# The triangular inverse of RWKV-7 as diagonal 32x32 blocks: four 32x32 tiles of the array instead of two 64x64

## The reference, cut to what matters

```python
def step(s, inp):
    r_t, w_t, kk_t, b_t, k_t, v_t = inp
    sa = jnp.einsum('dbhvk,dbhk->dbhv', s, kk_t)
    s = s * w_t[..., None, :] - sa[..., :, None] * b_t[..., None, :] + v_t[..., :, None] * k_t[..., None, :]
    return s, jnp.einsum('dbhvk,dbhk->dbhv', s, r_t)
```

## Time and profile before

| | value |
|---|---|
| median of the runs shown | 2692.78 us |
| time of the profiled execution | 2691.81 us |
| its span, first to last instruction | 2689.8 us |
| mean granted TensorE clock | 0.961 |
| the five turns of RWKV (from the first product of the ladder's operands) | 457.5 to 796.0 us |
| PE busy share of the span | 91% |

### The profile page before, as it was taken

How to read it: one execution, slowest core, us unless ns; L and a number is a source line. 1 busy time by engine, 2 the same in 40 slices (tenths; PEclk the granted TensorE clock), 3 DMA queues, 4 the chain that set the end, 5 groups by cost and what they waited for, 6 DMA issues and landing times.

```text
span 2689.8 us, 74227 instructions
## 1 busy us (share of the span) xinstructions
PE 2448.0 (91%) x34058; PEld 1706.7 (63%) x34058; DVE 601.4 (22%) x1164; ACT 536.0 (20%) x1037; POOL 217.9 (8%) x243
## 2 busy tenths in 40 slices
PE   5899985999999769999999899998794999999998
PEld 3555564999994466777666345457453777766654
DVE  1113456666652330000000010106315000000001
ACT  3111043444421310000000036114413000000000
POOL 2000020333300010000000000003001000000000
PEclk8999997999999889999999999999896999999999
DMA  7665300000012269999999311110014999999970
GB/s 282 191 216 180 132 1 14 4 4 4 4 44 68 108 248 373 397 397 396 396 394 392 115 50 47 48 63 32 16 58 159 353 392 397 396 394 394 396 274 39
DMA packets 173468, 529.19 MB, mean 197 GB/s; under 512 B 23124, under 2 KB 27888, under 8 KB 173296
## 3 DMA queue, kind: packets, MB, share of 16 engines
q1 hardware_dynamic: 158688, 489.45, 48.1%
q10 hardware_dynamic: 10336, 24.21, 3.1%
q0 software_dynamic: 4272, 12.91, 1.4%
HBM read 506.75 MB, written 11.40 MB: 193 GB/s over the span
## 4 chain that ended last, share of the span: by engine, by line
PE 68%; issue 16%; DMA 5%; DVE 3%; ACT 2%; POOLq 1%; ACTq 1%; DVEq 1%; POOL 1%; SPq 0%
PE ps L1710 19%; PE ps L1725 17%; PE ps L1124 7%; PE ps L458 4%; PE ps L1840 4%; DMA big<-w_exp_down 3%; PE ps L1209 2%; PE ps L1912 2%; PE ps L1134 2%; PE ps L1908 2%; PE ps L460 1%; PE ps L830 1%; PE ps L438 1%; PE ps L1703 1%; PE ps L1196 1%
## 5 line engine op out<-in xcount | busy, mean ns | idle before, releaser
L1710 PE MATMUL ps<-rs,ring 128*64 128x80 f32 x12288 | 441.8, 233 | 5.8 <-issue 5.5
L1710 PEld LDWEIGHTS ps<-rs,ring 128*64 128x64 f32 x12288 | 429.9, 137 | 23.9 <-issue 23.0
L1811 DVE TENSOR_TENSOR big<-big,ps 128x320 f32<-128x320 f32 x64 | 28.3, 483 | 993.8 <-PE ps L1725 954.8
L1725 PE MATMUL ps<-big 128*80 128x512 f32 x512 | 226.4, 595 | 1.9 <-DMA big<-w_exp_down 1.5
L1725 PE MATMUL ps<-ring,big 128*80 128x512 f32 x512 | 225.0, 592 | 2.4 <-DVE big L1811 2.4
L555 PE MATMUL ps<-hT,ring 128*128 128x512 f32 x336 | 176.1, 606 | 11.1 <-ACTq L602 11.1
L1124 PE MATMUL ps<-big 64*64 64x64 f32 x5440 | 166.5, 219 | 16.9 <-DVEq L1095 16.9
L1781 ACT COPY big<-ps 80x512 f32<-80x512 f32 x64 | 34.1, 582 | 711.0 <-PE ps L1725 711.0
L1124 PEld LDWEIGHTS ps<-big 64*64 64x64 f32 x5440 | 163.1, 136 | 18.2 <-DVEq L1095 17.2
L1725 PEld LDWEIGHTS ps<-ring,big 128*80 128x80 f32 x512 | 76.6, 150 | 145.9 <-issue 141.8
L1725 PEld LDWEIGHTS ps<-big 128*80 128x80 f32 x512 | 74.3, 150 | 131.5 <-issue 129.8
(11 more groups left out here) (392 smaller groups left out, 3002.1 us busy)
## 6 DMA issues: line engine op xcount, KB each, us to landing
ring<-w_exp_up SPq DMA_DIRECT2D x124, 1024.0 KB, 10.8
ring<-w_exp_gate SPq DMA_DIRECT2D x68, 1024.0 KB, 12.1
big<-w_exp_down SPq DMA_DIRECT2D x64, 1024.0 KB, 11.3
ring<-w_exp_down SPq DMA_DIRECT2D x64, 1024.0 KB, 11.5
big<-w_exp_gate SPq DMA_DIRECT2D x60, 1024.0 KB, 10.6
big<-w_ada SPq DMA_DIRECT2D x22, 2048.0 KB, 8.7
ring<-w_in_odd SPq DMA_DIRECT2D x6, 2048.0 KB, 8.9
big<-big ACTq DMA_DIRECT2D x32, 256.0 KB, 6.4
```

The lines of the kernel that those rows point to most:

```text
L1710: last = nc.tensor.matmul(ps[2 * m + j // 4][a:a + HALF, (j % 4) * SLOTS:(j % 4 + 1) * SLOTS], ex_blocks[ex_slot(q)][:, k % 2, j * P + a:j ...
L1725: last = nc.tensor.matmul(ps[4 + f][0:SLOTS, :], hid[:, k, :], ex_blocks[ex_slot(q)][:, k % 2, f * W:(f + 1) * W], start=(k == 0), stop=(k ...
```

## The change

A diagonal 32x32 block of L is inverted by levels 1 to 4 alone; only level 5 joins two of them to 64x64. The change keeps L, X, XT, T1 and the masks as these diagonal blocks: four 32x32 blocks stand on the four quarters of the partitions (`QUARTERS`), 8 of them side by side, 256 columns in place of 512. Levels 1 to 4 run as `quarters`, 32 matmuls of 32x32 with 32 columns, on four tiles of the array in turn; `each` ran 16 of 64x64 with 64 columns. The pair products are formed as blocks from the start (`pair_quarters`): the two diagonal blocks of each matrix, and the corner block that only level 5 uses. At level 5 `corner_left` multiplies the corner with X (16 matmuls), ACT takes the product over with a minus sign, and `corner_right` (32 matmuls) makes the joined corner and, by an identity, moves the second diagonal block beside it; DVE assembles the 64-wide `XTf`. The mask of level 5 goes, and the masks, copies and subtractions of levels 0 to 4 are 256 wide. The constants shrink by 414 columns.

```diff
-        T1 = MT
-        TbT, TkT, Lm, X, XT = ([wr.three(RB, N) for _ in BOTH] for _ in range(5))
-        Phi, Hm = Lm, X
-        Sc1 = [x[:, 0:RC, :] for x in XT]
+        T1 = [m[:, RB * N:RB * (N + QN)].rearrange("p (b t) -> p b t", b=RB) for m in LT_MT]
+        TbT, TkT, Phi, Hm, XTf = ([wr.three(RB, N) for _ in BOTH] for _ in range(5))
...
+        QUARTERS = [slice(QN * g, QN * (g + 1)) for g in range(4)]
...
+                def quarters(b, lhs, rhs):
+                    for j in range(RB):
+                        for g in QUARTERS:
+                            last = nc.tensor.matmul(ps[b][g, narrow(j)], lhs[g, j, :], quarter_ident[g, :] if rhs is None else rhs[g, j, :],
+                                                    start=True, stop=True)
+                    return last
+                def pair_quarters(e):
+                    for j in range(RB):
+                        for h in range(2):
+                            for q in range(2):
+                                nc.tensor.matmul(ps[4 * e + 1][QUARTERS[2 * h + q], narrow(j)], Bst[e][HALVES[h], j, QUARTERS[q]],
+                                                 Ast[e][HALVES[h], j, QUARTERS[q]], start=True, stop=True)
+                    for j in range(RB):
+                        for h in range(2):
+                            last = nc.tensor.matmul(ps[4 * e + 1][QUARTERS[2 * h + e], narrow(j, RB * QN)], Bst[e][HALVES[h], j, QUARTERS[e]],
+                                                    Ast[e][HALVES[h], j, QUARTERS[1 - e]], start=True, stop=True)
+                    return last
+                def corner_left(e):
+                    for j in range(RB):
+                        for h in range(2):
+                            last = nc.tensor.matmul(ps[4 * e + 1][QUARTERS[2 * h + 1 - e], narrow(j)], corner[e][QUARTERS[2 * h + e], j, :],
+                                                    X[e][QUARTERS[2 * h + e], j, :], start=True, stop=True)
+                    return last
+                def corner_right(e):
+                    for j in range(RB):
+                        for h in range(2):
+                            g = QUARTERS[2 * h + 1 - e]
+                            nc.tensor.matmul(ps[4 * e + 3][QUARTERS[2 * h + e], narrow(j)], T1[e][g, j, :], XT[e][g, j, :], start=True, stop=True)
+                            last = nc.tensor.matmul(ps[4 * e + 3][g, narrow(j)], quarter_ident[g, :], XT[e][g, j, :], start=True, stop=True)
+                    return last
...
                 for e in BOTH:
-                    each(4 * e + 1, Bst[e], Ast[e]).then_inc(sem("pairs_done"), 1)
+                    pair_quarters(e).then_inc(sem("pairs_done"), 1)
...
-                    turned(4 * e + 1, blocks_of(Lm[e])).then_inc(sem("x_product"), 1)
+                    quarters(4 * e + 1, Lm[e], None).then_inc(sem("x_product"), 1)
...
-                        each(4 * e + 1, Lm[e], X[e]).then_inc(sem("lx_done"), 1)
+                        if lv < LEVELS - 1:
+                            quarters(4 * e + 1, Lm[e], X[e]).then_inc(sem("lx_done"), 1)
+                        else:
+                            corner_left(e).then_inc(sem("lx_done"), 1)
...
-                            each(4 * e + 2, XT[e], T1[e]).then_inc(sem("x_product"), 1)
+                            quarters(4 * e + 2, XT[e], T1[e]).then_inc(sem("x_product"), 1)
                         else:
-                            each(4 * e + 3, T1[e], XT[e]).then_inc(sem("xt_product"), 1)
+                            corner_right(e).then_inc(sem("xt_product"), 1)
...
-                        nc.scalar.copy(T1[e], bank(4 * e + 1)).then_inc(sem("lx_kept"), 1)
+                        if lv < LEVELS - 1:
+                            nc.scalar.copy(T1[e], narrow_bank(4 * e + 1)).then_inc(sem("lx_kept"), 1)
+                        else:
+                            nc.scalar.mul(T1[e], narrow_bank(4 * e + 1), -1.0).then_inc(sem("lx_kept"), 1)
...
-                    if lv < LEVELS - 1:
+                    if lv < LEVELS - 2:
                         for e in BOTH:
                             dve.wait_ge(sem("lx_done"), n * 2 * (LEVELS - 1) + (2 * (lv - 1) + e + 1))
...
+                    for e in BOTH:
+                        if lv == LEVELS - 1:
+                            if e == 0:
+                                dve.drain()
+                            nc.vector.tensor_scalar(XTf[e][:, :, QUARTERS[e]], XT[e], quarter[:, e:e + 1], None, ALU.mult)
                     for e in BOTH:
                         dve.wait_ge(sem("xt_product"), n * 2 * (LEVELS - 1) + (2 * (lv - 1) + e + 1))
-                        nc.vector.tensor_tensor(XT[e], XT[e], bank(4 * e + 3), ALU.subtract).then_inc(sem("xt_updated"), 1)
+                        if lv < LEVELS - 1:
+                            nc.vector.tensor_tensor(XT[e], XT[e], narrow_bank(4 * e + 3), ALU.subtract).then_inc(sem("xt_updated"), 1)
+                        else:
+                            nc.vector.tensor_copy(XTf[e][:, :, QUARTERS[1 - e]], narrow_bank(4 * e + 3)).then_inc(sem("xt_updated"), 1)
```

More of the change, by code:

```diff
@@ L31 @@
 LEVELS = 6
+QN = 32
 W = 512
@@ L48 @@
                       ("rot", P), ("cos", TS), ("sin", TS), ("edges", 2 * P),
-                      ("chain", 512), ("strict", 2 * N), ("within", 2 * N), ("level", 2 * LEVELS * N),
+                      ("chain", 512), ("strict", 2 * N), ("within", 2 * N), ("level", 2 * (LEVELS - 1) * QN), ("quarter_ident", QN), ("quarter", 2),
                       ("half_ident", N),
@@ L101, in constants @@
     lv = []
-    for h in [2 ** i for i in range(LEVELS)]:
+    s, tt = p[:, None] % QN, np.arange(QN)[None, :]
+    for h in [2 ** i for i in range(LEVELS - 1)]:
         same = s // (2 * h) == tt // (2 * h)
@@ L106, in constants @@
     put("level", np.stack([np.stack(x, 1) for x in lv], 2))
+    put("quarter_ident", s == tt)
+    put("quarter", p[:, None] % N // QN == np.arange(2)[None, :])
     put("half_ident", np.concatenate([np.eye(N), np.eye(N)], 0))
@@ L942, in build @@
         rwkvc = wr(ROWS0 - RWKV0)
-        chain, strict, within, level, half_ident = (const(n, rwkvc, RWKV0) for n in ("chain", "strict", "within", "level", "half_ident"))
+        chain, strict, within, level, half_ident, quarter_ident, quarter = (const(n, rwkvc, RWKV0) for n in (
+            "chain", "strict", "within", "level", "half_ident", "quarter_ident", "quarter"))
         ones_less_ka = wr(4)
@@ L953, in build @@
         LT_MT = [wr(2 * RB * N) for _ in BOTH]
-        LT = [m[:, 0:RB * N].rearrange("p (b t) -> p b t", b=RB) for m in LT_MT]
+        LT, corner = ([m[:, x * RB * QN:(x + 1) * RB * QN].rearrange("p (b t) -> p b t", b=RB) for m in LT_MT] for x in range(2))
         MT = [m[:, RB * N:2 * RB * N].rearrange("p (b t) -> p b t", b=RB) for m in LT_MT]
         nWG = [m.rearrange("p (b t) -> p b t", b=RB) for m in LT_MT]
-        T1 = MT
-        TbT, TkT, Lm, X, XT = ([wr.three(RB, N) for _ in BOTH] for _ in range(5))
-        Phi, Hm = Lm, X
-        Sc1 = [x[:, 0:RC, :] for x in XT]
+        T1 = [m[:, RB * N:RB * (N + QN)].rearrange("p (b t) -> p b t", b=RB) for m in LT_MT]
+        TbT, TkT, Phi, Hm, XTf = ([wr.three(RB, N) for _ in BOTH] for _ in range(5))
+        Lm = [m.rearrange("p b t -> p (b t)")[:, 0:RB * QN].rearrange("p (b t) -> p b t", b=RB) for m in Phi]
+        X, XT = ([m.rearrange("p b t -> p (b t)")[:, x * RB * QN:(x + 1) * RB * QN].rearrange("p (b t) -> p b t", b=RB) for m in Hm] for x in range(2))
+        Sc1 = [x[:, 0:RC, :] for x in XTf]
         nr = Region(0, ring0, 2 * KC * W)
@@ L1026, in bank, with narrow_bank @@
             return ps[b][:, :].rearrange("p (b t) -> p b t", b=RB)
+        def narrow_bank(b):
+            return ps[b][:, 0:RB * QN].rearrange("p (b t) -> p b t", b=RB)
         def prepare_lora_pe(turn, e, pe):
@@ L1125, in each, with narrow @@
                     return last
+                def narrow(j, right=0):
+                    return slice(right + QN * j, right + QN * (j + 1))
+                def quarters(b, lhs, rhs):
[28 more added lines that the diff above has]
+                    return last
                 def blocks_of(x):
@@ L1147, in rwkv_pe @@
                 for e in BOTH:
-                    pe.wait_ge(sem("level_masked"), n * 2 * LEVELS + (e + 1))
-                    turned(4 * e + 1, blocks_of(Lm[e])).then_inc(sem("x_product"), 1)
+                    pe.wait_ge(sem("level_masked"), n * 2 * (LEVELS - 1) + (e + 1))
+                    quarters(4 * e + 1, Lm[e], None).then_inc(sem("x_product"), 1)
                 for e in BOTH:
@@ L1169, in rwkv_pe @@
                         pe.wait_ge(sem("x_updated"), n * 2 * (LEVELS - 1) + (2 * (lv - 1) + e + 1))
-                        pe.wait_ge(sem("level_masked"), n * 2 * LEVELS + (2 * lv + e + 1))
-                        each(4 * e + 1, Lm[e], X[e]).then_inc(sem("lx_done"), 1)
+                        if lv < LEVELS - 1:
```

(32 more changed lines are left out.)

## The result

The changed kernel takes 2830.7 us (median of four runs, 2827.24 to 2835.62) against 2692.0 for the kernel before in the same comparison: a ratio of 1.0514, 95% interval 1.0491 to 1.0537. That is 139 us slower where 2644 us was forecast, outside the range and on the other side.

What follows compares the result with a forecast made beforehand. PE, busy 337.9 of 338.5 us, was taken to bound the RWKV stage. Four turns gaining 10.2 us and a last gaining 10.8 made 51.6, less 0.5 a turn: 49 us, so 2644 us; range 2632 to 2735.

Steps and rivals of the forecast that it cites:

- the third rival: RWKV turns: instructions don't arrive in time, 25 transfers a turn instead of 17; at 3 us each 2728 us; chance 0.08.
- The price of a record: Matmuls on four 32x32 tiles: all four stream together, 7.9 ns a record, 0.51 us a call of 64.
- The first rival: PE's queue: matmuls follow each other no faster than 27 ns; +26.4 us a turn, 2824 us; chance 0.18.
- The levels: Ladder levels 1 to 4: 3.18 us each instead of 5.60, together -9.7 us a turn.
- the fourth rival: Ladder levels: semaphores between PE, ACT and DVE give back half the gain, 1 us a level; 2664 to 2690; chance 0.08.
- The wait for POOL ahead of phi: After level 5: ACT waits for POOL before L1275, so phi begins at 23.7 us after the ladder's start, not 23.3.
- The tile-shape excursions: Pair products, transpose of L and ladder: three added tile-shape changes per turn, 0.33 us each, 1.0 us.

Runs made afterwards that it cites:

- e1: Changed kernel with six extra matmul stretches ahead of the RWKV turns, three shapes, straight and looped; four tiles: straight 128 records per 3.4 to 4.0 us, looped 64 in 0.886.
- e2: Kernel before, tiles kept at 64x64, with each ladder product of 64 columns cut into two of 32; 2823.6 us, ratio 1.0492.
- e3: Changed kernel with levels 1 to 4 of the ladder as one loop on TensorE instead of straight code; 2711.4 us, ratio 1.0077.

## Why the prediction was wrong

**The failed step** is the third rival, "Instructions don't arrive": "A transfer occupies 1.6% x 16 x 339 / 84 = 1.03 us, 26 us a turn, well hidden", and "I take it as hidden. Chance 0.08." It took the time that a transfer occupies DMA engines for the time between transfers. The rival's other numbers were right: 25 transfers a turn, deciding from 2.7 us, and at 4.0 us each a loss of 160. With the 3.73 us of e1 (ten bursts from 445.18 to 482.47 us) it gives 25 x 3.73 - 68 = 25 us a turn, 126 in five, with the 3.87 us of the stage 144; 139 was measured. The 1.03 us was read rightly: in e1 each transfer of q8 is under way for 0.9 to 1.3 us. But none overlaps another, there or in the kernels before and after, and most of the time between two passes with none under way:
```profile
GB/s 0 17 0 0 0 17 0 0 0 17 0 0 17 0 0 8 17 0 0 0 17 0 0 17 0 0 0 0 17 0 0 0 17 0 0 0 17 0 0 0
q8 instruction: 10, 0.16, 1.6%
```
These are 445 to 484 us of e1 in slices of 0.975 us (the 8 is another queue's). A burst begins 1.3 to 1.5 us after a transfer has ended, and the next transfer begins 1.0 to 1.7 us after the start of the burst. So a transfer costs a cycle of 3.73 us on average, of which only the 0.9 to 1.3 us show as DMA time. The profile before had one pace for this, 4.0 us, and no row with a faster one (in its trace no transfer of q8 starts within 3.3 us of the one before); PE was busy all the time, so a pace that just kept up looked like one with room. As the nearest row it belonged in the range, and the range left it out.

**The price of a record**, on which "decides nearly everything" was said, held nearly: 7.9 ns was forecast, 8.8 measured. In the loops a pass of 384 records keeps PE busy 4.00 us, 10.4 ns each with the tail of each call, and ten calls of e1 keep it busy 7.53 us for 640, 11.8 ns; each of them contains the 0.2 us that a matmul itself lasts. Without it, (0.753 - 0.2) / 63 = 8.8 ns. So four 32x32 tiles do stream together, and a call's records begin within 0.55 us, where 0.51 was forecast. The reason was only half right: columns alone do not set the price, since halving them on 64x64 tiles saved nothing (e1, e2). What counts there is the width of the weights, as the corner products of the changed kernel show (L1157, granted clock 1.00).
```profile
552.27 0.60 PE L1157 MATMUL ps<-big 64*32 64x32 f32 x28
```
They have 64 rows, 32 moving columns and two tiles, as the records of e2, but weights (and an output) of 32 columns in place of 64. 28 of them begin within 0.60 - 0.19 = 0.41 us, 15 ns each, half of e2's 29.5 and close to the 15.7 that the prediction had for them.

The Trainium skill, "TensorE: Matmul & The Clock Gate", section "Wait — 56ns, not 53.3ns?", says that two matmuls start no nearer than about 25 ns, however few columns they have. The looped call of e1, 64 records in 0.886 us with its jump, contradicts that across four tiles. The first rival, built on 27 ns, falls by the same call, though its time (2824) came nearest: 128 x 27 ns is 3.46 us, so a record floor and a transfer limit give nearly the same total, and only the burst pattern and the loop tell them apart.

**The levels** were put at 3.18 us. Passes at full clock take 4.32 and 4.22 (the windows of e3); 0.2 to 0.3 us of idle a pass stands at the jump and the waits there, and the rest is 8.8 for 7.9 ns and the tails. So at most 0.3 of the 1 us a level of the fourth rival is there.

**The wait for POOL ahead of phi** does not show: PE reaches phi so late that ACT's copy ahead of it waits for PE's product (L1332 for L1250, 32.8 us in ten times) and not for POOL. It is not refuted, only covered. The tile-shape excursions (1.0 us a turn) were not told apart. **The clock** was not forecast to move. It fell with PE's idle time, and the products with AMV rose from 5 x 3.60 us to 26.9 in all (L1250). Behind the ladder, where PE does not wait, the second turn takes 20.0 us (627.34 to 647.35, clock 0.94) where it took 18.8 (577.34 to 596.10, clock 1.00): about 1.2 us a turn, 6 of the 139, are the clock's. It does not set the pace of the bursts: in e1 the burst of 1.38 us (clock 0.86) and those of 1.93 us (0.50) are followed alike, 3.4 to 4.0 us after their start, by the next.

The Trainium skill, "Runtime: NRT & Kernel Launch", section "Instruction fetch mechanics", says that instructions come in blocks of 256, that crossing into the next is mostly hidden, and that a taken branch can cost a fetch, one reason why kernels prefer full unrolling. The block size agrees with the bursts of 128 records; the rest does not hold here: the crossing cost 1.5 to 2.6 us in e1, and the loop gained 119 us.

## What to carry to other kernels

Before records are made smaller and more, count instructions per microsecond of straight code and compare with the fastest pace of instruction transfers that the profile has shown, not with the share of DMA time that they take; 128 records with their loads per 3.75 us is about where this kernel already stood. Idle time put down to "issue" after equal counts of instructions is the sign. A loop takes such a stretch out of the limit (shown here for a body of 384 records, three transfers), but nearly all of the code behind it is fetched only when it ends, so the transfers outside the loop and the later passes add up.

## What was not expected of the hardware

- One transfer of 256 instructions per 3.4 to 4.0 us on TensorE, whatever the clock and with the DMA engines nearly idle (share 0.02). In the traces one transfer follows the other and none overlaps; why the next does not begin earlier stays open.
- A loop over one call costs 0.32 us a jump more than the records (0.886 us for 64 records at 8.8 ns, 0.56), 0.13 of it idle, and no transfer falls in it.
- A matmul record on 64x64 tiles takes 29.2 ns with 32 columns as with 64; on two tiles with 32 columns of weights 15; on four 32x32 tiles, with 32 columns, 8.8.
- An instruction that does nothing, put behind each matmul in threes, added 66 ns each, and the granted clock of that stretch fell from 1.00 to 0.50 although PE shows as busy.
